# A decoder step on one core: its 344 weight tiles fetched as one 1 MB transfer each in place of two of 512 KB

## The chip, the cores and the metric

The kernel runs on one core of one Trainium2 chip. The metric is the time of one execution on the device in microseconds (us), the median of three runs.

## The reference

One inference step of a one-layer decoder, for 256 prompt tokens and 8 sample tokens, width 2048, all in float32:

```
h    = rmsnorm(x);  proj = h @ w_in                    # 2048 x 7168: conv parts b, c, h and q, k, v, g of 8 heads
y    = [ b * causal_conv3(c*h),  silu(g) * groupnorm(retention(rotary(q), rotary(k), v)) ]
x    = x + y @ w_out                                   # 2048 x 2048
xb   = rmsnorm(x);  q = xb @ w_q                       # 8 heads x 2 x 128
i1, i2 = top16(q0 @ keys0), top16(q1 @ keys1);  best = top16(v1 + v2)   # per token and head
out  = x + sum over the 8*16 picks of softmax(best) * gelu(xb . u[idx]) * v[idx],   idx = 128*i1 + i2
y    = rmsnorm(out);  new conv and retention states are returned too
```

u and v have 16384 rows of 2048. The kernel doesn't gather rows: it multiplies all tokens with all of u, weighs the result with the gates (zero where an expert isn't picked), and multiplies with all of v.

## The kernel before, in words

**Tiles and halves.** All weights (w_in, w_out, w_q, u, v) lie in one DRAM array `halves`, in the order of use. A tile is 16 blocks of 128 x 128 float32, 1 MB; it consists of two halves of 8 blocks, 512 KB, each stored as [128 partitions][8][128], so 4 KB in one piece for a partition. There are 344 tiles, 688 halves, and every half passes once through four steps:

- SP (the queue of `block.sync`) fetches it into one of `RING` = 4 places of `raw` (L520, the first four halves at L504).
- ACT casts it to its high part `whi` (`hi_half`, L607 to L612), once the transfer has landed (`raw_full[s]`) and TensorE has used the half that lay in that place of `whi` before (`half_used`).
- DVE subtracts, raw - whi, to get the low part `wlo` (`lo_half`, L1137), and counts `lo_done`.
- TensorE (`half`, L874 to L884) waits for `lo_done` and runs 24 matmuls of 264 columns: high weight by high and by low activation, low weight by high activation (L881, L882, L883), and counts `half_used`.

**What sets the order.** Nothing is scheduled by a tool: each engine runs a list written out by hand. ACT and DVE call `ahead(r, k)`, which makes the halves 2k+2 and 2k+3 after the tile k is on TensorE, and between two such calls they do the work of the stage: in the eight heads rotation, retention and group norm; then the short convolution; the output projection; queries and scores; then routing (top 16, decoding), and gates, gelu, weighing, and adding. Each engine runs strictly in its order, so what stands behind a cast that waits for its transfer waits too. SP's list is the loop of `fetch` alone after the start: for half m it waits until `lo_done` reaches m - 3, that is, until the low part of half m - 4, which lay in that place, is made.

**The start.** SP issues the norm gains, four blocks of the input x (`acc`, 528 KB each) and halves 0 to 3 between them, and a table (`keep`), then the loop. GpSimd (POOL) waits for the last block of x and then fetches the tables (1584 KB), small constants and the first states (512 KB) over a queue of its own. ACT's list there is `first_squares` (L667 to L682):

```
hi_half(0, 2); hi_half(0, 3)
for c in range(CH):  square of chunk c      # after c == 7: hi_half(0, 4)
hi_half(0, 5); hi_half(0, 6)
root_of_sum(1)
hi_half(0, 7)
ahead(0, 3)                                 # halves 8 and 9
```

and only behind it come the first head's `swap(1)` and `swap(2)` (L644 to L646), which exchange the two halves of k and q for the rotation. DVE's list in the first head (`first_norm`, L1185, and `head`, L1289) makes the low parts of halves 4, 5, 6 and 7 between sums of the squares, then the rotations `rotate(kT...)` and `rotate(qT...)` (L1210 to L1218), then the low parts of halves 8 and 9. On TensorE `turn` (L924), the transposes of v and k for the retention of head 0, comes after tile 3 (halves 6 and 7) and before tile 4 (halves 8 and 9), and waits for both rotations (`rot_ready`).

Of the kernel before, what the change touches and what calls it, by code (L numbers as in the profile page):

```python
# [43 lines left out]
RING = 4  # L44
# [168 lines left out]
def build(nc, halves, xT, conv_state, ret_state, norm_mix, conv_w, gn_g, gn_b, norm_ffn, keysT, norm_fin,  # L213
          consts, out_yT, out_conv, out_pret, out_sret):
    with ExitStack() as ctx:
        def sb(name, shape, dt=F32, scope=ctx):
            return scope.enter_context(nc.sbuf_tensor(name, shape, dt))

        def sem(name):
            return ctx.enter_context(nc.semaphore(name))  # L220


        raw = sb("raw", [P, RING, HALF, P])
# [156 lines left out]
        raw_full = [sem(f"raw_full{s}") for s in range(RING)]  # L380
        hi_done = sem("hi_done")
        lo_done = sem("lo_done")
# [107 lines left out]
        def u_tile(g):  # L490
            return W_U0 if isinstance(g, int) and g == 0 else W_MAIN + (g - 1) * TILES_ROUND

        def v_tile(g):
            last = isinstance(g, int) and g == GROUPS - 1
            return W_MAIN + g * TILES_ROUND + (0 if last else GROUP)


        @block.sync
        def _(sp):
            def x_block(c):  # L500
                sp.dma_start(acc[:, 4 * c:4 * c + 4, :], xT[:, 4 * c:4 * c + 4, :]).then_inc(x_in[c], 16)

            def first_half(s):
                sp.dma_start(raw[:, s], halves[s]).then_inc(raw_full[s], 16)  # L504

            sp.dma_start(gains[:, 0, :], norm_mix).then_inc(gain_in, 16)
            x_block(0)
            first_half(0)
            x_block(1)
            x_block(2)  # L510
            first_half(1)
            x_block(3)
            first_half(2)
            sp.dma_start(keep[:], consts[:, 0:KEEP]).then_inc(keep_in, 16)
            first_half(3)

            def fetch(n, at):
                for s in range(RING):
                    sp.wait_ge(lo_done, n + s - (RING - 1))
                    sp.dma_start(raw[:, s], halves[at + s]).then_inc(raw_full[s], 16)  # L520

            turns = 2 * GROUP // RING
            with sp.Fori(1, 2 * (C_LEAD + GROUP) // RING) as r:
                fetch(r * RING, r * RING)
            with sp.Fori(1, LEAD) as g:
                for i in range(turns):
                    fetch(2 * (C_LEAD + g * GROUP) + i * RING, 2 * u_tile(g) + i * RING)
            with sp.Fori(0, MIXED) as g:
                n = 2 * (C_MAIN + g * TILES_ROUND)
                for i in range(turns):  # L530
                    fetch(n + i * RING, 2 * u_tile(g + LEAD) + i * RING)
                for i in range(turns):
                    fetch(n + 2 * GROUP + i * RING, 2 * v_tile(g) + i * RING)
            with sp.Fori(MIXED, GROUPS - 1) as g:
                for i in range(turns):
                    fetch(2 * (C_TAIL + (g - MIXED) * GROUP) + i * RING, 2 * v_tile(g) + i * RING)
            g = GROUPS - 1
            for i in range(turns):
                fetch(2 * (C_TAIL + (g - MIXED) * GROUP) + i * RING, 2 * v_tile(g) + i * RING)
            for b, (c, n) in enumerate(FINAL):  # L540
                sp.wait_ge(y_out, b + 1)
                sp.dma_start(out_yT[:, c:c + n, :], acc[:, c:c + n, :]).then_inc(stored, 16)
            sp.wait_ge(stored, len(FINAL) * 16)
            sp.wait_ge(conv_stored, 16)
            sp.wait_ge(st_stored, 32 * HEADS)
# [59 lines left out]
        def _(act):  # L605
            def hi_half(r, off):

                s = off % RING
                act.wait_ge(raw_full[s], 16 * (r + off // RING + 1))
                if not (isinstance(r, int) and RING * r + off < RING):  # L610
                    act.wait_ge(half_used, RING * r + off - (RING - 1))
                nc.scalar.copy(whi[:, s], raw[:, s]).then_inc(hi_done, 1)  # L612

            def ahead(r, k):

                hi_half(r, 2 * k + 2)
                hi_half(r, 2 * k + 3)
# [40 lines left out]
            for c in range(CH):  # L658
                if c % 4 == 0:
                    act.wait_ge(x_in[c // 4], 16)  # L660
                times_gains(0, c)
                if c == 3:
                    hi_half(0, 0)
                if c == 11:
                    hi_half(0, 1)
# [143 lines left out]
            for n in range(LEAD_TILES):  # L809
                r, k = C_LEAD // 2, n  # L810
# [49 lines left out]
            r = C_TAIL // 2 + (GROUPS - 1 - MIXED) * (GROUP // 2)  # L860
# [997 lines left out]
```

## Time and profile before

| what | before |
|---|---|
| runs shown | 2143.92 us median of 3 (2143.17 to 2144.35) |
| the profiled execution | 2143.7 us, its span 2142.1 us |
| granted TensorE clock, mean | 0.998 |
| busy: PE / DVE / ACT / POOL | 99% / 66% / 44% / 3% of the span |
| DMA | 414.17 MB, mean 193 GB/s |
| weights, SP's queue | 688 transfers of 512 KB, 3.5 us from issue to landing at the median |

Read the busy shares first, then the chain of work that ended last: both say which engine sets the end. An engine that isn't in the chain may be busy or idle at no cost. For a transfer the question is not how long it takes but whether an engine waited for it, and whether TensorE waited for that engine. In a timeline the brackets at a row's end give how long its engine was idle before it, and who ended that.

### The profile page before, as it was taken

What the parts mean: (1) busy time and instruction counts of PE and PEld (TensorE: products, weight loads), DVE (VectorE), ACT (ScalarE), POOL (GpSimd) and SP (SyncE); (2) the same over time, 40 slices, a digit from 0 to 9 for tenths busy, and PEclk for the clock granted to TensorE, in tenths of its full rate; (3) what the DMA queues carried; (4) which work ended last, traced back from release to release, by engine and by line L of the source; (5) the groups of instructions that cost most, each with busy time, mean ns of one, the idle gap of its engine ahead of it and who ended that gap; (6) DMA issues with size and microseconds to landing.
All of it is one profiled execution on the core that took longest, in us unless ns stands there. A gap on an engine that the chain in (4) does not pass through costs nothing.

```text
span 2142.1 us, 46352 instructions
## 1 busy us (share of the span) xinstructions
PE 2119.1 (99%) x18553; PEld 2101.1 (98%) x18553; DVE 1421.5 (66%) x2684; ACT 941.1 (44%) x1303; POOL 59.7 (3%) x78
## 2 busy tenths in 40 slices
PE   8999999999999999999999999999999999999997
PEld 7999999999999999999999999999999999999997
DVE  7667776568888667754656566666655556666665
ACT  6454433444444434444434343444434344444444
POOL 1000000000010000000000000000000000000000
PEclk9999999999999999999999999999999999999999
DMA  7555555654455556675656665656656566666553
GB/s 276 178 188 179 181 166 179 201 184 151 154 188 181 184 173 217 208 237 194 201 183 213 193 215 184 212 194 201 205 194 202 178 206 212 205 209 206 199 178 127
DMA packets 113767, 414.17 MB, mean 193 GB/s; under 512 B 13216, under 2 KB 13728, under 8 KB 113344
## 3 DMA queue, kind: packets, MB, share of 16 engines
q1 hardware_dynamic: 100800, 365.29, 52.6%
q0 software_dynamic: 8480, 30.24, 4.4%
q10 hardware_dynamic: 4320, 16.22, 1.9%
q8 instruction: 128, 2.10, 0.4%
q14 instruction: 39, 0.32, 0.0%
HBM read 387.36 MB, written 24.26 MB: 192 GB/s over the span
## 4 chain that ended last, share of the span: by engine, by line
PE 98%; DVE 1%; ACT 0%; DMA 0%; issue 0%; DVEq 0%; SPq 0%; ACTq 0%
PE bank L881 31%; PE bank L882 31%; PE bank L883 31%; PE bank L1058 2%; PE bank L959 1%; PE bank L1013 1%; PE bank L948 0%; PE bank L969 0%; DVE wlo L1137 0%; DMA acc<-xT 0%; PE bank L946 0%; DVE acc L1785 0%; PE bank L936 0%; PE bank L965 0%; ACT whi L612 0%
## 5 line engine op out<-in xcount | busy, mean ns | idle before, releaser
L1137 DVE TENSOR_TENSOR wlo<-raw,whi 128x1024 fp32r<-128x1024 f32 x688 | 829.9, 1223 | 537.7 <-ACT whi L612 534.4
L612 ACT CAST whi<-raw 128x1024 fp32r<-128x1024 f32 x688 | 709.6, 1048 | 646.0 <-PE bank L883 636.8
L881 PE MATMUL bank<-xhi,whi 128*128 128x264 f32 x3200 | 911.5, 285 | 0.0
L882 PE MATMUL bank<-xlo,whi 128*128 128x264 f32 x3200 | 906.7, 283 | 0.0
L883 PE MATMUL bank<-xhi,wlo 128*128 128x264 f32 x3200 | 906.5, 283 | 0.0
L882 PEld LDWEIGHTS bank<-xlo,whi 128*128 128x128 f32 x3200 | 603.1, 188 | 0.0
L881 PEld LDWEIGHTS bank<-xhi,whi 128*128 128x128 f32 x3200 | 602.6, 188 | 0.2 <-issue 0.2
L883 PEld LDWEIGHTS bank<-xhi,wlo 128*128 128x128 f32 x3200 | 600.1, 188 | 0.0
L881 PE MATMUL bank<-xghi,whi 128*128 128x264 f32 x1152 | 333.6, 290 | 11.2 <-DVE wlo L1137 11.2
L881 PE MATMUL bank<-wexp_hi,whi 128*128 128x264 f32 x1152 | 328.0, 285 | 0.0
L882 PE MATMUL bank<-xglo,whi 128*128 128x264 f32 x1152 | 327.4, 284 | 0.0
L883 PE MATMUL bank<-xghi,wlo 128*128 128x264 f32 x1152 | 327.0, 284 | 0.0
L882 PE MATMUL bank<-wexp_lo,whi 128*128 128x264 f32 x1152 | 326.4, 283 | 0.0
L883 PE MATMUL bank<-wexp_hi,wlo 128*128 128x264 f32 x1152 | 326.1, 283 | 0.0
L881 PEld LDWEIGHTS bank<-xghi,whi 128*128 128x128 f32 x1152 | 217.9, 189 | 18.0 <-DVE wlo L1137 10.1
L882 PEld LDWEIGHTS bank<-xglo,whi 128*128 128x128 f32 x1152 | 217.8, 189 | 0.4
L882 PEld LDWEIGHTS bank<-wexp_lo,whi 128*128 128x128 f32 x1152 | 217.0, 188 | 0.0
L881 PEld LDWEIGHTS bank<-wexp_hi,whi 128*128 128x128 f32 x1152 | 217.0, 188 | 0.0
L883 PEld LDWEIGHTS bank<-xghi,wlo 128*128 128x128 f32 x1152 | 216.9, 188 | 0.0
L883 PEld LDWEIGHTS bank<-wexp_hi,wlo 128*128 128x128 f32 x1152 | 216.0, 187 | 0.0
L791 ACT ACTIVATE hid<-bank 128x264 f32<-128x264 f32 x128 | 49.8, 389 | 205.3 <-PE bank L883 203.9
L1729 DVE TENSOR_TENSOR acc<-bank,acc 128x264 f32<-128x264 f32 x256 | 99.3, 425 | 49.3 <-PE bank L883 49.3
(215 smaller groups left out, 1102.2 us busy)
## 6 DMA issues: line engine op xcount, KB each, us to landing
raw<-halves SPq DMA_DIRECT2D x688, 512.0 KB, 3.5
hid<-gates ACTq DMA_DIRECT2D x30, 528.0 KB, 4.6
gates<-stage POOLq DMA_DIRECT2D x17, 768.0 KB, 7.1
s_old<-ret_state POOLq DMA_DIRECT2D x8, 512.0 KB, 6.0
ret_sample<-s_new POOLq DMA_DIRECT2D x8, 512.0 KB, 4.1
gates<-route_mem POOLq DMA_DIRECT2D x5, 768.0 KB, 7.2
acc<-xT SPq DMA_DIRECT2D x4, 528.0 KB, 6.4
tables<-shape_constants POOLq DMA_DIRECT2D x1, 1584.0 KB, 8.3
```

The costliest lines, as they stand in the source:

```text
L612: nc.scalar.copy(whi[:, s], raw[:, s]).then_inc(hi_done, 1)
L791: nc.scalar.activation(hid[:, slot_of(g, k)], bank[b][:, 0:T].unsqueeze(1), ACT.Gelu)\
L881: nc.tensor.matmul(out, whi[:, s, c], mh[c], start=start and c == 0, stop=False)
L882: nc.tensor.matmul(out, whi[:, s, c], ml[c], start=False, stop=False)
L883: mm = nc.tensor.matmul(out, wlo[:, s, c], mh[c], start=False, stop=stop and c == HALF - 1)
L959: mm = nc.tensor.matmul(bank[6][:, NPROMPT + b:NPROMPT + b + 1], s_new[:, b], qT[:, NPROMPT + b:NPROMPT + b + 1], start=True, stop=True)
L1013: mm = nc.tensor.matmul(bank[4 + b][0:n, t * NK:(t + 1) * NK], qs[:, b, t0:t0 + n], keys_sb[:, j, :], start=True, stop=True)
L1058: mm = nc.tensor.matmul(o, onehot2[:, e, t], gated1[:, e, part, t], start=part == 0, stop=part == PARTS - 1)
L1137: v.tensor_tensor(wlo[:, s], raw[:, s], whi[:, s].bitcast(F32), ALU.subtract).then_inc(lo_done, 1)
L1729: v.tensor_tensor(acc[:, j, :], bank[off % BANKS][:, 0:T], acc[:, j, :], ALU.add)\
```

## The change

`fetch` walks the ring by two. One transfer fetches both halves of a tile, `raw[:, s:s + 2]`, in a pattern of 128 x 2 x 1024 elements (two pieces of 4 KB for each partition, 512 KB apart in DRAM), and counts on the semaphore of the even place alone. It begins when `lo_done` says that the odd half's place is free too. ACT's cast of an odd half waits for the even place's semaphore, except for halves 0 to 3, which still come one by one.

```diff
             def fetch(n, at):
-                for s in range(RING):
-                    sp.wait_ge(lo_done, n + s - (RING - 1))
-                    sp.dma_start(raw[:, s], halves[at + s]).then_inc(raw_full[s], 16)
+
+                for s in range(0, RING, 2):
+                    sp.wait_ge(lo_done, n + s + 1 - (RING - 1))
+                    sp.dma_start(raw[:, s:s + 2], halves[bass.ds(at + s, 2)].rearrange("s p c k -> p s c k"))\
+                        .then_inc(raw_full[s], 16)
...
             def hi_half(r, off):

                 s = off % RING
-                act.wait_ge(raw_full[s], 16 * (r + off // RING + 1))
+                alone = isinstance(r, int) and RING * r + off < RING
+                act.wait_ge(raw_full[s if alone else s - s % 2], 16 * (r + off // RING + 1))
```

The order of instructions on SP, the last transfer of the start and the first turn of the loop. Before:

```order
L504 DMA raw<-halves 128x1024
L523 UNCONDITIONAL_BRANCH
L523 ISA
L520 ISA [waits lo_done]
L520 DMA raw<-halves 128x1024
L519 REGISTER_ALU
L520 ISA [waits lo_done]
L520 DMA raw<-halves 128x1024
```

With the change:

```order
L504 DMA raw<-halves 128x1024
L525 UNCONDITIONAL_BRANCH
L525 ISA
L521 ISA [waits lo_done]
L521 DMA raw<-halves 128x2x1024
L521 ISA [waits lo_done]
L521 DMA raw<-halves 128x2x1024
```

Each transfer of the loop carries two halves, and there is one wait for `lo_done` for the two.

The order on ACT at the start, from the cast of half 4 to the first swap. Before:

```order
L612 CAST whi<-raw 128x1024 [waits half_used,raw_full0]
L675 ACTIVATE squares<-acc 128x264 [waits sq_used] x8
L612 CAST whi<-raw 128x1024 [waits half_used,raw_full1]
L612 CAST whi<-raw 128x1024 [waits half_used,raw_full2]
L637 ACTIVATE stats<-bank 128x264 [waits sum_done]
L612 CAST whi<-raw 128x1024 [waits half_used,raw_full3]
L612 CAST whi<-raw 128x1024 [waits half_used,raw_full0]
L612 CAST whi<-raw 128x1024 [waits half_used,raw_full1]
L645 COPY swapped<-bank 64x264 [waits half_used]
```

With the change (the lines have moved down by three):

```order
L615 CAST whi<-raw 128x1024 [waits half_used,raw_full0]
L678 ACTIVATE squares<-acc 128x264 [waits sq_used] x8
L615 CAST whi<-raw 128x1024 [waits half_used,raw_full0]
L615 CAST whi<-raw 128x1024 [waits half_used,raw_full2]
L640 ACTIVATE stats<-bank 128x264 [waits sum_done]
L615 CAST whi<-raw 128x1024 [waits half_used,raw_full2]
L615 CAST whi<-raw 128x1024 [waits half_used,raw_full0] x2
L648 COPY swapped<-bank 64x264 [waits half_used]
```

No instruction has moved. The casts of halves 4, 5 and of halves 8, 9 now wait for one transfer each, and the swap still stands behind both casts of the second.

## Rows read from the trace of the kernel before

**Rows 1.** The page: part 1, busy time of each engine, and part 4, chain by engine

```profile
PE 2119.1 (99%) x18553; PEld 2101.1 (98%) x18553; DVE 1421.5 (66%) x2684; ACT 941.1 (44%) x1303; POOL 59.7 (3%) x78
...
PE 98%; DVE 1%; ACT 0%; DMA 0%; issue 0%; DVEq 0%; SPq 0%; ACTq 0%
```

**Rows 2.** Waits of PE: line waited for, us in total, times, longest us

```profile
PE bank L881 <- DVE wlo L1137: 11.2, 2, 9.8
PE bank L913 <- DVE stats L1183: 0.9, 1, 0.9
```

**Rows 3.** Windows (busy us of each engine, PEclk, DMA share, GB/s): a steady stretch

```profile
1570.00:1810.00 240.00, 240.00 (x1989) 240.00 (x1988) 134.01 (x180) 101.02 (x126) 0.00 (x0) 1.00 0.60 197
```

**Rows 4.** Tile raw, whole run: duration ns min/median/max, idle before it, landing

```profile
L612 ACT CAST whi<-raw x688: 1028/1047/1058, 7.5 to 2120.3; 128x1024 fp32r<-128x1024 f32 x172
L1137 DVE TENSOR_TENSOR wlo<-raw,whi x688: 1204/1224/1229, 8.6 to 2121.6; 128x1024 fp32r<-128x1024 f32 x172
...
  DMA raw<-halves: 8.0, 4
...
DMA to landing us min/median/max: 3.1/3.5/9.5
```

**Rows 5.** Tile raw, 119 to 122.5 us: halves 36 and 37, issued back to back

```profile
L520 SPq DMA_DIRECT2D raw<-halves x2: 332/332/333, 120.6 to 121.7; - x2
...
DMA to landing us min/median/max: 3.2/3.7/4.2
```

**Rows 6.** SP's issue of half 5; issues at 14.2 to 15 and 17 to 17.8, us to landing

```profile
14.34 0.34 SPq L520 DMA_DIRECT2D raw<-halves  x1
...
raw<-halves SPq DMA_DIRECT2D x1, 512.0 KB, 7.6
...
raw<-halves SPq DMA_DIRECT2D x1, 512.0 KB, 8.2
```

**Rows 7.** Windows of the start, DMA share and GB/s last

```profile
14.00:16.00 2.00, 2.00 (x18) 2.00 (x18) 2.00 (x6) 1.97 (x3) 2.00 (x5) 1.00 1.06 429
22.00:24.00 2.00, 2.00 (x19) 2.00 (x18) 1.68 (x3) 1.60 (x5) 0.00 (x0) 1.00 1.02 342
```

**Rows 8.** Timeline of ACT, start: start us, us, line, tile [idle before, releaser]

```profile
19.35 1.03 ACT L612 CAST whi<-raw 128x1024 fp32r<-128x1024 f32 x1
...
29.03 1.05 ACT L612 CAST whi<-raw 128x1024 fp32r<-128x1024 f32 x1 [0.22 <-DMA raw<-halves]
30.38 1.06 ACT L612 CAST whi<-raw 128x1024 fp32r<-128x1024 f32 x1 [0.30 <-PE bank L883]
31.46 0.38 ACT L645 COPY swapped<-bank 64x264 f32<-64x264 f32 x1
...
41.49 1.05 ACT L612 CAST whi<-raw 128x1024 fp32r<-128x1024 f32 x1 [3.63 <-DMA raw<-halves]
```

**Rows 9.** Timeline of DVE, start: low part of half 5, and qT

```profile
24.85 1.23 DVE L1137 TENSOR_TENSOR wlo<-raw,whi 128x1024 fp32r<-128x1024 f32 x1
...
35.43 0.43 DVE L1218 TENSOR_TENSOR qT<-qT,rot 128x264 f32<-128x264 f32 x1
```

**Rows 10.** Timeline of PE, start: first matmul of the turn

```profile
36.01 0.41 PE L928 MATMUL bank<-keep,vT 128*128 128x128 f32 x2
```

**Rows 11.** Timelines of SP, ACT and PE near 284 us

```profile
284.61 0.33 SPq L520 DMA_DIRECT2D raw<-halves  x1
...
286.89 1.06 ACT L612 CAST whi<-raw 128x1024 fp32r<-128x1024 f32 x1 [3.68 <-DMA raw<-halves]
...
283.45 0.36 PE L881 MATMUL bank<-xghi,whi 128*128 128x264 f32 x1 [1.37 <-DVE wlo L1137]
```

**Rows 12.** Windows at the first matmuls and at the end, granted clock after POOL

```profile
9.80:13.90 4.10, 4.05 (x18) 4.05 (x19) 4.10 (x9) 4.10 (x10) 1.36 (x3) 1.00 1.03 416
2131.00:2133.00 2.00, 0.80 (x4) 0.34 (x2) 0.71 (x2) 0.49 (x2) 0.00 (x0) 1.00 0.00 0
2133.00:2135.00 2.00, 0.00 (x0) 0.00 (x0) 1.93 (x4) 0.00 (x0) 0.00 (x0) 0.66 0.00 0
```

## The prediction

> **What bounds the kernel now.** I read the page first. TensorE is busy for 99% of the span, and the chain that ended last runs over it for 98% [rows 1]. Nothing that an engine, a queue or a transfer saves elsewhere shortens the span; only what makes TensorE wait, or wait less, counts. The waits of TensorE come next: two on a finished low part (DVE, L1137), together 11.2 us, 9.8 of which are the start before the first matmul, and 0.9 us at the end [rows 2]. So the weights arrive in time everywhere but once, for 1.4 us, and the change can win almost nothing. The question is where it makes TensorE wait.
>
> A steady stretch gives the pace: 1989 matmuls in 240.00 us, 0.1207 us each, 24 to a half, so 2.90 us for a half and 5.8 us for a tile [rows 3]. A half costs ACT 1.05 us (high part) and DVE 1.22 us (low part); a transfer lands in 3.5 us at the median and 9.5 at most, and in the whole run ACT's casts wait for a transfer four times, 8.0 us in all [rows 4]. Halves are numbered from 0 in their order of use.
>
> **What the change does to a transfer.** The even half of a pair no longer starts when its own place is free but when the odd one's is, and both are there only when 1 MB has landed. Nothing before half 4 is touched, and no instruction of PE, DVE, ACT or POOL moves; SP issues 342 transfers in place of 684. That saves 342 issues on a queue that only waits: nothing.
>
> No row has a 1 MB transfer on this queue, so its landing time is bounded. Two halves issued 1.13 us apart (120.6 and 121.7) took 3.2 to 4.2 us, so the pair was complete about 1.1 + 4.2 = 5.3 us after the first issue, 5.4 with rounding [rows 5]. That is the upper end. The lower end is the quiet single landing, 3.2 to 3.3 us, plus 0.5 MB at the 429 GB/s that the engines reached when full [rows 7], 1.2 us: 4.5 us. I take 4.9, between them, since one transfer has no second start but the same bytes. The Trainium skill (DMA: Bandwidth & Descriptors, "Anatomy of one DMA") gives a fixed 2.0 us and the bytes at 436 GB/s: 3.2 us for half a megabyte, with which the trace agrees, and 4.4 us for one; the sum below would be 0.5 us smaller by it. Its table of measured sizes on another issue path has 6.15 us for 1 MB, by which the sum would be 1.2 us larger; no row here has that size.
>
> **Steady stretches: nothing.** A place pair is held from the issue to the end of the second low part: the landing, 0.2 us of issue, two casts and one low part, 1.0 + 1.0 + 1.2, so 4.9 + 3.4 = 8.3 us. There are two such pairs and TensorE eats one in 5.8 us, so each may take 11.6 us. 3.3 us are left. The one place after the start where ACT waited for a transfer is half 80: half 81 was issued at 284.61, half 80 just before it, and the cast of half 80 began at 286.89 [rows 11]. As a pair they land near 284.6 + 4.9 = 289.5, and the low part of half 80 ends at 289.5 + 2.3 = 291.8. TensorE started half 76 at 283.45 and reaches half 80 four halves later, at 295.1. The 1.4 us wait ahead of half 76 hangs on a chain of DVE work and stays.
>
> **The start: this is the term.** The places are filled while inputs and constants crowd the same engines.
> - Halves 4 and 5. Half 5 is issued at 14.34 as before, half 4 (at 9.97 before) now with it. Half 5 landed 7.6 us later, at 21.9; half 6, issued at 17.09, took 8.2 and landed at 25.3 [rows 6]. The engines are full from 14 to 16 us (share 1.06, 429 GB/s), and move 342 GB/s from 22 to 24 [rows 7]. With full engines the same bytes pass whichever goes first, so the pair is complete near 21.9. Below: 0.5 MB less stands ahead of the constants and all come 1.2 us sooner, 20.7. Above: it shares with 0.5 MB more at 342 GB/s, 1.5 us later, 23.4. I take 22.1, since GpSimd's constants, issued from 12.5, get the room that half 4 leaves.
> - ACT casts half 4 at 19.35 now [rows 8]. It does so at 22.1, 2.75 us later. Behind that cast in ACT's order stand eight squares and the cast of half 5, behind it on DVE the sums of the squares. The low part of half 5 ended at 24.85 + 1.23 = 26.08 [rows 9], 6.7 us after the cast of half 4 began, with hardly a gap between; so it ends at 28.8. TensorE waits for these two halves, 1 to 2 us in all.
> - Halves 8 and 9 are issued when that low part ends: 28.8 + 0.2 = 29.0. Half 8 alone went out after the low part of half 4 and was there at 29.03 [rows 8]. The pair lands at 29.0 + 4.9 = 33.9, with a quiet queue, since half 6 is in at 25.3 and half 7, the 9.5 us of [rows 4], soon after.
> - ACT casts halves 8 and 9 ahead of the two half-swaps of the first head (L645). Before, the casts began at 29.03 and 30.38 and the first swap at 31.46 [rows 8]; now the casts begin at 33.9 and 34.9 and the swap at 35.9, 4.4 us later. DVE's rotation waits for it: qT was ready at 35.43 + 0.43 = 35.86 [rows 9], and TensorE's turn (L928) began at 36.01, the moment it was [rows 10]. There was no room at all. DVE's multiply stood 1.0 us behind the first swap because of other work, now long done; 0.4 us of the 4.4 come back.
> - Sum for TensorE: 22.1 + 6.7 + 0.2 + 4.9 = 33.9, less 29.9: the 29.03 of the old cast, the 0.5 us that shrink between cast and swap (2.4 before, when the cast of half 9 waited for TensorE, 2.0 now) and the 0.4 that come back. That is +4.0 us. With both lower ends +2.2 (20.7 and 4.5), with both upper ends +5.8 (23.4 and 5.4).
> - Halves 12 and 13 are issued after the low part of half 9, which follows the rotation: 40.0 + 2.4 = 42.4, landed at 47.5, half 12 cast and its low part made by 49.8 (its cast began at 41.49 [rows 8]). TensorE starts half 8 after the turn, past 41 now, and half 12 four halves later, not before 52.6: nothing added.
>
> TensorE never has idle time later in which to catch up, so the 4.0 us stay to the end. The profiled execution took 2143.7 us beside a span of 2142.1 and a median of the runs of 2143.92, the same within 0.01%. 2143.9 + 4.0 = **2147.9 us**, +0.19%. A difference of 0.2%, 4.3 us, is about what a measurement of this kernel can tell from none; the forecast lies just inside it.
>
> **Rivals.**
> 1. Slower by more than 0.2%: the same mechanism with a late pair. It decides once landing time of halves 4 and 5 and the quiet landing together exceed 27.3 us (22.1 + 4.9 = 27.0 in the forecast). For it: half 6 landed only at 25.3, since GpSimd's transfers took turns with it. Against it: they are through sooner. With 23.4 and 5.4 it gives +5.8, 2149.7 us.
> 2. The stall cools the clock. At the end TensorE's last matmul lies in 2131 to 2133, at the full clock (2.4 GHz); in 2133 to 2135 the granted mean is 0.66, so it fell to half (1.2 GHz) 0.6 us into that stretch, within 2.6 us of work [rows 12]. The new wait near 38 us is the rest of the 4.0, 2 to 3 us. For it: that may be as long. Against it: the 1.4 us gap near 283 was followed by the full clock, and here the work before and after is dense. At the start 18 matmuls took 4.10 us, 0.228 each [rows 12], 0.107 more than in the steady stretch (that row grants 1.00, but the pace is that of the lower level); 18 of them again are +1.9: 2149.8 us.
> 3. Steady starvation. If the pair needed 9 us, the places would be held 9 + 3.4 = 12.4 of 11.6 us, 0.8 too much for each of 172 double tiles: +138 us, 2282 us. From 8.2 us it decides. For it: the longest single landing is 9.5. Against it: that one is in the crowd of the start, and the median is 3.5.
> 4. No loss, or a gain. Either the pair is split so that its first half is as early as before, or larger transfers are much quicker. The Trainium skill (same page, "Rules for kernel authors") asks for at least 1 MiB in a transfer for full bandwidth. On the rows, quicker landings could win back the 1.4 us near 283 at most: 2142.5 to 2143.9 us.
>
> **How the numbers follow.** Forecast 0.50, rival 1 0.32, rival 2 0.05, rival 3 0.05, rival 4 0.08 (0.05 of it no difference, 0.03 faster by an unseen way). Slower by over 0.2%: 0.32 + 0.05 + 0.05 = 0.42; within: 0.50 + 0.05 = 0.55; faster: 0.03. The range starts at the lower ends, +2.2, rounded to 2146.0, and takes in the upper ends with the clock, 5.8 + 1.9 = 7.7: 2151.6. Rivals 3 and 4, 0.13, lie outside.
>
> **What would show it.** The cast of half 4 at 22 with a wait on the transfer in place of 19.35; the casts of halves 8 and 9 near 34, with some 4 us of waiting; waits of TensorE of 1 to 2 us on low parts between 23 and 29, and one of 2 to 3 us at the turn (L928, three lines lower in the new file) that ends near 40; landings of 4.6 to 5.4 us at the median; every stretch after 60 us as long as before. I am wrong if TensorE waits on low parts in later stretches, if the median landing is above 6 us, or if the first head starts its turn before 38 us.

## The result, and the profile after

| what | before | with the change |
|---|---|---|
| runs | 2143.92 us median of 7 (2143.17 to 2144.35) | 2149.83 us median of 7 (2149.39 to 2151.58) |
| the profiled execution | 2143.7 us, span 2142.1 us | 2149.74 us, span 2148.2 us |
| granted TensorE clock, mean | 0.998 | 0.997 |

The ratio is 1.003, with an interval of 1.0019 to 1.0041: 5.9 us slower, 0.28%. The forecast said 4.0, the range 2.1 to 7.7; the time is that of rival 1, the late pair. It is also past the 0.2% within which the prediction expected the change to stay (0.55, against 0.42 for slower than that). Five of the seven runs lie within 1.3 us (2149.39 to 2150.63), two at 2151.45 and 2151.58.

The waits of PE in the changed kernel (line waited for, us in total, times, longest us), against [rows 2]:

```profile
PE bank L884 <- DVE wlo L1140: 14.3, 3, 9.7
PE bank L931 <- DVE qT L1221: 1.5, 1, 1.5
PE bank L916 <- DVE stats L1186: 0.9, 1, 0.9
```

One wait on a low part has been added and one on the rotation. The window of [rows 3] and a longer one up to the end of the weights, with the granted clock before the last two numbers:

```profile
1570.00:1810.00 240.00, 240.00 (x2006) 239.95 (x2005) 133.02 (x177) 100.99 (x126) 1.16 (x1) 1.00 0.58 198
590.00:2130.00 1540.00, 1539.53 (x13881) 1535.33 (x13881) 997.90 (x1739) 663.12 (x875) 35.22 (x40) 1.00 0.58 197
```

TensorE is as full as before (2006 matmuls against 1989: a few per cent of the records can be missing). So nothing is lost later, and all of the loss lies in the first 42 us. There the chain reads, on ACT (start us, us, line, tile, and in brackets how long ACT was idle before it and who ended that):

```profile
23.89 1.04 ACT L615 CAST whi<-raw 128x1024 fp32r<-128x1024 f32 x1 [4.64 <-DMA raw<-halves]
28.33 1.99 ACT L615 CAST whi<-raw 128x1024 fp32r<-128x1024 f32 x2
...
35.63 2.00 ACT L615 CAST whi<-raw 128x1024 fp32r<-128x1024 f32 x2 [2.41 <-DMA raw<-halves]
37.65 0.38 ACT L648 COPY swapped<-bank 64x264 f32<-64x264 f32 x1
```

on DVE, where the two low parts at 29.39 are those of halves 5 and 6:

```profile
24.97 1.23 DVE L1140 TENSOR_TENSOR wlo<-raw,whi 128x1024 fp32r<-128x1024 f32 x1 [4.80 <-ACT whi L615]
29.39 2.36 DVE L1140 TENSOR_TENSOR wlo<-raw,whi 128x1024 fp32r<-128x1024 f32 x2
...
38.51 0.43 DVE L1218 TENSOR_TENSOR kT<-bank,tables 128x264 f32<-128x264 f32 x1 [1.52 <-ACT swapped L649]
...
41.49 0.43 DVE L1221 TENSOR_TENSOR qT<-qT,rot 128x264 f32<-128x264 f32 x1
```

and on PE:

```profile
26.25 0.39 PE L884 MATMUL bank<-xghi,whi 128*128 128x264 f32 x1 [3.25 <-DVE wlo L1140]
...
31.49 0.48 PE L884 MATMUL bank<-xghi,whi 128*128 128x264 f32 x1
...
42.07 0.41 PE L931 MATMUL bank<-keep,vT 128*128 128x128 f32 x2 [1.53 <-DVE qT L1221]
```

The turn began at 36.01 [rows 10] and begins at 42.07: +6.06. Every half from 8 on is 6.05 to 6.08 us later, and the span is 6.1 us longer.

The two landings that the sum of the prediction holds, from the DMA issues of 14 to 15 us and of 30.5 to 31.5 us (KB, us to landing):

```profile
raw<-halves SPq DMA_DIRECT2D x1, 1024.0 KB, 9.7
...
raw<-halves SPq DMA_DIRECT2D x1, 1024.0 KB, 4.8
```

And tile `raw` in the whole run, us to landing:

```profile
DMA to landing us min/median/max: 4.7/4.9/9.8
```

The quiet landing is 4.9 us, as taken. That of halves 4 and 5 is 9.7, from 14.15 to 23.87, where 7.8 (14.34 to 22.1) was taken. Why it is so long is in the queues' shares of the engines (queue, packets, MB, share of 16 engines; q1 is SP's, q0 GpSimd's), of 14.5 to 18 us, then 18 to 21, then 21 to 24:

```profile
q0 software_dynamic: 102, 1.29, 92.7%
q1 hardware_dynamic: 4, 0.00, 0.3%
...
q1 hardware_dynamic: 208, 0.85, 74.4%
q0 software_dynamic: 206, 0.26, 24.8%
...
q0 software_dynamic: 142, 0.50, 53.4%
q1 hardware_dynamic: 141, 0.51, 47.7%
```

GpSimd issued its tables (1584 KB) at 12.32, the pair was issued at 14.15, and for almost four microseconds it moved hardly a byte. About two of these four a pair takes even alone. The quiet pair 8/9 was issued at 30.80, and these are its rows of 31 to 32, 32 to 33 and 33 to 34 us:

```profile
q1 hardware_dynamic: 13, 0.05, 68.0%
q1 hardware_dynamic: 28, 0.11, 41.9%
q1 hardware_dynamic: 110, 0.45, 109.3%
```

It was in full flow 2.2 us after its issue. From 18 to 21 us the pair 4/5 had three quarters of the engines, and from 21 on about half, beside the first states, which GpSimd had issued at 16.21. The engines weren't full all the time either. The window of 14 to 16 us, where half 4 was among what passed before (429 GB/s, [rows 7]), now reads:

```profile
14.00:16.00 2.00, 2.00 (x19) 2.00 (x18) 2.00 (x5) 2.00 (x3) 2.00 (x5) 1.00 1.03 337
```

**The clock.** The windows from TensorE's wait before half 4 to the end of the next halves:

```profile
22.90:26.50 3.60, 0.34 (x3) 0.26 (x3) 1.53 (x2) 2.31 (x5) 0.00 (x0) 1.00 0.84 305
26.50:29.90 3.40, 3.40 (x17) 3.40 (x17) 2.94 (x5) 2.96 (x6) 0.00 (x0) 0.50 0.02 8
29.90:33.00 3.10, 3.10 (x24) 2.96 (x23) 2.50 (x4) 1.53 (x3) 0.00 (x0) 1.00 0.35 54
```

After 3.25 us without a matmul, the granted clock was 0.50 for 3.40 us, which is 1.2 GHz. In the timeline the matmuls of that stretch begin 0.22 us apart (the count of 17 takes in those that its edges cut), where 0.12 is usual. In this execution that costs little: TensorE waits for qT at the turn in any case, and what half 4 took longer (half 5 is late by 4.45 us where half 4 was by 2.81, so 1.6) is missing from the wait at the turn, 1.5 instead of about 3.

### The profile page after: what moved, and what is told of

Its sections match the earlier page's. It is cut to its first block, busy times and chain, and to the rows that moved or that the text cites. A ratio compares the mean times of both kernels' runs of the same rounds, so it can differ in the third digit from the quotient of the medians.

```text
span 2148.2 us, 45008 instructions
## 1 busy us (share of the span) xinstructions
PE 2120.6 (99%) x18553; PEld 2102.3 (98%) x18553; DVE 1421.3 (66%) x2684; ACT 940.7 (44%) x1303; POOL 59.7 (3%) x78
## 4 chain that ended last, share of the span: by engine, by line
PE 97%; DVE 1%; DMA 1%; ACT 0%; issue 0%; DVEq 0%; SPq 0%; ACTq 0%
PE bank L884 31%; PE bank L885 31%; PE bank L886 30%; PE bank L1061 2%; PE bank L962 1%; PE bank L1016 1%; DMA raw<-halves 0%; DVE wlo L1140 0%; PE bank L951 0%; PE bank L972 0%; DMA acc<-xT 0%; ACT whi L615 0%; PE bank L949 0%; DVE acc L1788 0%; PE bank L939 0%
```

## The experiments

Every kernel was timed beside the kernel before on the same chip; before had medians of 2143.91 (e1 to e4), 2144.03 (e5 to e8) and 2143.81 (e9 to e12). The theory: the whole loss is made at the start, by two links in a chain, the pair 4/5 that comes late and the pair 8/9 whose casts stand ahead of the swaps. The rivals: it is made in the steady part by tight places; or it is the clock; or a single one of the two links makes it.

### Where: the steady part or the start

In e1 and e2 `fetch` chooses between a pair and two single halves, each with the wait of its own kernel, and ACT's wait follows it (`one` and `two` hold the two forms of the transfer; SP's first two turns stand ahead of its loop). e1 begins with pairs at half 12; e2 has pairs for halves 4 to 11 alone.

```diff
+            def fetch(n, at, first=()):
+                for s in range(0, RING, 2):
+                    if (n + s in FIRST) if isinstance(n, int) and n < 3 * RING else STEADY:
+                        sp.wait_ge(lo_done, n + s + 1 - (RING - 1))
+                        two(s, at)
+                    else:
+                        for t in (s, s + 1):
+                            sp.wait_ge(lo_done, n + t - (RING - 1))
+                            one(t, at)
```

> Pairs from half 12 on only; halves 4 to 11 come one by one as before. Start theory (the whole loss is made by the pairs 4/5 and 8/9): no difference from before, 2143.9 +- 0.5 us, no wait of TensorE beside the three of before. Rival (part of the loss is spread over steady stretches): +0.5 us or more, with new waits of TensorE on low parts after 60 us.

Measured: 2143.7 us (2143.14 to 2144.59, 11 runs), ratio 0.9999 (0.999 to 1.0008). ACT's waits for a transfer (whole run) grow from 4 to 20 and cost nothing, since PE's are those of [rows 2] but for 0.1 us:

```profile
ACT whi L634 <- DMA raw<-halves: 53.9, 20, 6.5
PE bank L903 <- DVE wlo L1159: 11.3, 2, 9.9
```

So 338 pairs change the time by no more than 0.1% either way. The steady rival falls.

> Pairs for halves 4 to 11 only, singles from half 12 on. Start theory: all of the loss, +5.9 us, 2149.8, with the wait before half 4 and the wait at the turn as in the changed kernel. Rival of a spread loss: clearly less than +5.9.

Measured: 2150.4 us (2148.62 to 2151.37), ratio 1.0029 (1.0019 to 1.0039): four pairs are the whole loss. In its profile the clock fell in another place. The turn's first matmul,

```profile
41.59 0.41 PE L950 MATMUL bank<-keep,vT 128*128 128x128 f32 x2 [2.28 <-DVE qT L1240]
```

and the windows from before the turn to half 9:

```profile
36.00:42.90 6.90, 4.62 (x39) 4.41 (x38) 4.23 (x11) 4.63 (x8) 0.00 (x0) 1.00 0.33 135
42.90:46.30 3.40, 3.40 (x17) 3.40 (x17) 3.40 (x5) 0.52 (x2) 0.00 (x0) 0.51 0.62 181
```

Here nothing waits behind the slow stretch. The halves are 5.6 us late before it and 7.1 after it, so this time the clock is on the path, for 1.5 us. That is rival 2 as the prediction described it.

### Which pair

e3 has `FIRST = (4,)` and e4 `FIRST = (8,)` in the same code, all others single.

> Only halves 4 and 5 come as a pair. They land near 23.9 us, TensorE starts half 5 4.4 us later than before, and the cast of half 8 waits for nothing, since half 8 goes out after the low part of half 4 (26.2) and is there near 30. Theory of two links (late 4/5, then late 8/9): +4.4 if the half-rate clock after the wait is repeated, +2.8 if it is not. Rival (4/5 alone does it all): +5.9.

Measured: 2147.6 us (2146.93 to 2148.75), ratio 1.0018 (1.0009 to 1.0027): +3.7, between the two values expected (2.8 and 4.4). In its profile the clock stayed full.

> Only halves 8 and 9 come as a pair, issued after the low part of half 5, 26.07 + 0.2 = 26.3, landed 4.9 later at 31.1. The cast of half 8 begins 2.1 us later than before and 0.4 to 0.5 of that comes back at the swap: theory of two links +1.5 to +1.6 us, with one wait of TensorE at the turn. Rival (the landing has room here): 0.

Measured: 2145.3 us (2144.95 to 2145.43), ratio 1.0006 (0.9997 to 1.0016): +1.4, which the interval does not tell from nothing; the trace does. ACT's casts of halves 8 and 9, then the first swap, in e4:

```profile
31.16 2.00 ACT L634 CAST whi<-raw 128x1024 fp32r<-128x1024 f32 x2 [2.11 <-DMA raw<-halves]
33.18 0.38 ACT L667 COPY swapped<-bank 64x264 f32<-64x264 f32 x1
```

The swap stood at 31.46 [rows 8]: 1.7 us earlier. The pair was issued at 26.28, after the low part of half 5, and half 8 alone had gone out after that of half 4. So the two links are worth 3.7 and 1.4, and together 5.9 or 6.5, some 1 us over their sum.

### Late start, or larger transfer

e5 keeps the change's wait but sends two single halves.

```diff
-                    sp.dma_start(raw[:, s:s + 2], halves[bass.ds(at + s, 2)].rearrange("s p c k -> p s c k"))\
-                        .then_inc(raw_full[s], 16)
+                    for t in (s, s + 1):
+                        sp.dma_start(raw[:, t], halves[at + t]).then_inc(raw_full[t], 16)
```

> Every tile comes as two transfers of 512 KB with a semaphore each, but both are issued when both places are free: the late start without the one large transfer. Half 4, issued at 14.2, lands when half 5 did before, near 21.9, half 5 near 23.7; the low part of half 5 ends near 28.6, half 8 lands 3.3 us after its issue at 28.8, half 9 near 33.4, and the first swap comes near 34.5 in place of 31.46. Start theory: +2.9 us (2146.8): the late start and the size each carry about half of the loss. Rival (the late start is all): +5.9. Rival (the size is all): 0.

Measured: 2146.16 us (2145.75 to 2146.92), ratio 1.0009 (1.0 to 1.0019): +2.1, expected 2.9. The casts of half 4, then of halves 8 and 9:

```profile
21.89 1.05 ACT L614 CAST whi<-raw 128x1024 fp32r<-128x1024 f32 x1 [2.45 <-DMA raw<-halves]
...
32.09 1.05 ACT L614 CAST whi<-raw 128x1024 fp32r<-128x1024 f32 x1 [2.11 <-DMA raw<-halves]
33.38 1.05 ACT L614 CAST whi<-raw 128x1024 fp32r<-128x1024 f32 x1 [0.23 <-DMA raw<-halves]
```

The cast of half 4 went from 19.35 to 21.89 by the later start and from there to 23.89 by waiting for 1 MB: 2.5 and 2.0 us. In the profiled execution (2146.58 us) the turn begins at 38.88, 2.9 us late. So a third to a half of the whole loss is the later start (2.1 to 2.9 of 5.9), the rest the size of what is waited for.

### Taking the links away, one by one

e6 takes the casts of halves 8 and 9 out of the way of the swaps; all transfers stay pairs.

```diff
                 hi_half(0, 7)
-                ahead(0, 3)
...
-                if loads_tiles(h) and not first:
+                if loads_tiles(h):
                     ahead(r, 3)
```

> The changed kernel, with ACT's casts of halves 8 and 9 put behind the two half-swaps of the first head. The pair 8/9 still lands near 35.5, but the rotation no longer waits for it. Theory (the loss of the second pair goes through ACT's order): what is left is the late pair 4/5, as in the run that paired only these, +3.7 us, 2147.6; the wait at the turn falls under 0.5 us. Rival (TensorE would wait for half 8 itself): +5.9.

Measured: 2147.93 us (2146.75 to 2148.79), ratio 1.0018 (1.0009 to 1.0027): +3.9. TensorE's wait at the turn fell to 0.2 us. What is left is the price of the pair 4/5, as in e3.

e7 makes GpSimd wait with its tables until halves 0 and 4/5 are in.

```diff
-            pool.wait_ge(x_in[3], 16)
+            pool.wait_ge(raw_full[0], 32)
```

> The changed kernel, with GpSimd's first transfers (tables, constants, first states, 2.2 MB) held back until halves 4 and 5 have landed. Theory (the pair is late because it shares the engines with them): it lands in 5 to 5.5 us, near 19.5 in place of 23.9, its cast is on time, and only the second pair is late, 26.4 + 4.9 to 7 us: +1.8 to +3.8 us, 2146.1 likeliest. Rival (the wait for both places is the cause, not the company): the pair lands at 23 or later and the loss stays at +5.9.

Measured: 2148.94 us (2148.33 to 2150.11), ratio 1.0022 (1.0012 to 1.0032): +4.9. The time is a miss, the reading of the crowd is not. Landings of the pairs 4/5 and 8/9 (issued at 13.83 and 25.75):

```profile
raw<-halves SPq DMA_DIRECT2D x1, 1024.0 KB, 4.8
...
raw<-halves SPq DMA_DIRECT2D x1, 1024.0 KB, 8.0
```

ACT's cast of half 8 and the first matmul of the turn:

```profile
33.76 1.99 ACT L615 CAST whi<-raw 128x1024 fp32r<-128x1024 f32 x2 [5.79 <-DMA raw<-halves]
...
40.20 0.64 PE L931 MATMUL bank<-keep,vT 128*128 128x128 f32 x2 [4.90 <-DVE qT L1221]
```

and the windows up to the start of half 8, and of half 8:

```profile
36.00:42.20 6.20, 2.00 (x10) 1.91 (x11) 4.91 (x10) 3.26 (x6) 0.00 (x0) 0.84 0.01 3
42.20:45.90 3.70, 3.70 (x27) 3.70 (x27) 3.70 (x8) 0.52 (x2) 0.00 (x0) 0.81 0.67 205
```

With GpSimd's transfers out of its way, the pair 4/5 takes 4.8 us where it took 9.7, and half 4 is no longer late. But the tables now meet the pair 8/9, which takes 8.0, and TensorE waits 4.9 us at the turn in one piece. The rotation waited for the swap and not for the tables that it reads: DVE waited 4.3 us for the swap there, and 0.5 us for GpSimd's constants, by 30.17. The clock falls there too: 0.84 and 0.81 are 1.0 us and 0.7 us less than full, as 3.4 us at half would make them, and half 8 takes 3.7 us in place of 3.0.

e9 joins both edits: the tables late and the swaps ahead.

> The changed kernel with both repairs: GpSimd's first transfers after halves 4 and 5, and ACT's casts of halves 8 and 9 behind the two half-swaps. The pair 4/5 lands near 18.7 as in the run with late tables, the pair 8/9 near 33.7 (it meets the tables), in time for a cast that begins near 34. Theory (the loss consists of these two waits and nothing else): 2144.0 to 2145.0, the time of before plus 0 to 1 us. Rival (something else in the pairs costs time at the start): +2 us or more.

Measured: 2143.68 us (2143.12 to 2144.94), ratio 1.0 (0.9991 to 1.001), with pairs everywhere. PE's waits on low parts, then ACT at the start:

```profile
PE bank L883 <- DVE wlo L1139: 11.4, 2, 10.0
```

and

```profile
19.53 1.03 ACT L615 CAST whi<-raw 128x1024 fp32r<-128x1024 f32 x1
...
29.29 0.38 ACT L648 COPY swapped<-bank 64x264 f32<-64x264 f32 x1
```

Half 4 is cast at 19.53 without a wait and the swap no longer stands behind a transfer. The loss is gone, within the 2 us that the interval allows, and the trace has no wait of TensorE left at the start after the first matmul: the two links are all of it. The two repairs weren't run with single halves, but there they have no wait to remove, since TensorE doesn't wait between its first matmul and 283 us before the change [rows 2].

### The clock's part

e8 runs 12 matmuls that nothing reads before half 4 and 12 before head 1's turn in PE's list, that is, in the two waits. They are extra work.

```diff
+                    if first and k == 2:
+                        pe.wait_ge(keep_in, 16)
+                    if first and k == 2 or isinstance(h, int) and h == 1 and k == 0:
+                        for _ in range(12):
+                            nc.tensor.matmul(bank[7][:, 0:P], ones, ident, start=True, stop=True)
```

> The changed kernel, with 12 small matmuls into an unused bank ahead of half 4 and 12 ahead of the first turn (extra work, its results are not read). They fill some 2.6 us of the two waits. Theory (the runs of the changed kernel above 2150 us are those in which the clock fell in the wait at the turn and half 8 ran at half rate): no stretch at half clock before the end, no run above 2150.2, the median 2149.5. Rival (the spread comes from the landing of the transfers): the spread stays, 2149.4 to 2151.6.

Measured: 2149.89 us (2149.41 to 2150.79, 8 runs), ratio 1.0027 (1.0016 to 1.0038). The window of its start:

```profile
22.00:45.00 23.00, 22.62 (x185) 21.84 (x184) 16.11 (x27) 13.01 (x23) 0.00 (x0) 1.00 0.45 154
```

The clock stayed at 1.00 (2.4 GHz) throughout, and the median is that of the changed kernel. The expected values, a median of 2149.5 and no run above 2150.2, were both missed: two of the eight runs lie above (2150.30 and 2150.79). So the clock is no part of the typical loss; the chain of transfers, casts and rotation sets it, whatever TensorE does meanwhile. The highest run came down from 2151.58 to 2150.79, but the runs still spread over 1.4 us. That the two slowest runs of the changed kernel are those in which the clock fell on the path, as in e2's profile, fits, but with eight runs it isn't shown.

### What could still be won, and how near the edge is

The wait of 1.4 us ahead of half 76 is there in both kernels. e10 is the kernel before with DVE's low parts of halves 76 and 77 at the head of their channel's work instead of near its end; e11 is e9 with the same.

```diff
                 conv_ahead(3 * j)
+                if j == 1:
+                    conv_ahead(3 * j + 2)
...
-                conv_ahead(3 * j + 2)
+                if j != 1:
+                    conv_ahead(3 * j + 2)
```

> The kernel before (singles), with DVE's low parts of halves 76 and 77 put at the head of the second channel of the convolution in place of its middle. They are ready near 281 in place of 283.3, and the one wait of TensorE in mid-run, 1.4 us near 283, goes. Theory: -1.2 to -1.4 us, 2142.7. Rival (the channel's chain is late next and the wait moves behind it): 0.

> The changed kernel (pairs) with both repairs of the start and the early low parts of halves 76 and 77. If the three act apart: the time of the run with both repairs less 1.2 to 1.4 us, about 2143, the same as the singles with early low parts within 1 us. If larger transfers had a gain of their own anywhere, it would lie below these singles.

Measured: e10 2142.05 us (2141.55 to 2143.29, 11 runs), ratio 0.9992 (0.9983 to 1.0001), 1.8 us less than before; e11 2142.62 us (2141.5 to 2143.04, 11 runs), ratio 0.9993 (0.9984 to 1.0002). The intervals just reach 1, but in e10's trace the wait is gone:

```profile
PE bank L881 <- DVE wlo L1137: 10.1, 1, 10.1
```

With pairs or with single halves the repaired kernel takes the same time within 0.6 us. Pairs bring nothing of their own.

e12 begins every pair one half later.

```diff
-                    sp.wait_ge(lo_done, n + s + 1 - (RING - 1))
+                    sp.wait_ge(lo_done, n + s + 2 - (RING - 1))
```

> The changed kernel, with every pair begun one half later still (it waits for the low part of the next half too). In stages where ACT casts the next tile only when TensorE has finished one, that half comes a whole tile later, 5.8 us: a place is then held 4.9 + 3.4 + 5.8 = 14.1 us, of 11.6 that there are. Theory of the margin (3.3 us in the changed kernel, and 2.5 too much here): 2.5 us for each of 172 double tiles, +430 us, near 2570. Rival (the margin is much larger than 3.3 us): under +100 us.

Measured: 2655.03 us (one run), +511 us where +430 was expected. The half that it now waits for lies in the other pair of places, so a pair can't start before the one ahead of it has landed. The casts of three pairs in a row:

```profile
1604.58 2.00 ACT L615 CAST whi<-raw 128x1024 fp32r<-128x1024 f32 x2 [4.94 <-DMA raw<-halves]
1612.05 2.00 ACT L615 CAST whi<-raw 128x1024 fp32r<-128x1024 f32 x2 [5.47 <-DMA raw<-halves]
1619.96 1.99 ACT L615 CAST whi<-raw 128x1024 fp32r<-128x1024 f32 x2 [5.43 <-DMA raw<-halves]
```

and the window of [rows 3]:

```profile
1570.00:1810.00 240.00, 204.04 (x1783) 198.87 (x1779) 119.62 (x188) 78.67 (x106) 4.61 (x4) 0.97 0.47 160
```

That is a pair every 7.5 us or more, where TensorE eats one in 5.8. The mean clock is 0.97 in this window, so it falls in some of the waits too. Starvation in every tile, as rival 3 has it, would look like this, though here the pairs are kept apart and their landing is as quick as before; the change itself keeps clear of it by the one half.

## Why the prediction was right, and where it was short

- **Steady stretches: nothing.** Right, and shown by e1 (2143.7 against 2143.91). The slowest pair took 8.3 us in 1570 to 1810 us, past the 8.2 from which rival 3 would decide if all did; the 3.3 us of room that each pair has carried it.
- **342 issues saved: nothing.** Right: the same e1, and e11 against e10.
- **The quiet landing, 4.9 us.** Right to 0.1: 4.8 for the pair 8/9, 4.9 at the median. By the formula of the Trainium skill (DMA: Bandwidth & Descriptors, "Anatomy of one DMA") it would have been 4.4, and by its table 6.15. The page gives both for transfers issued from GpSimd, and these are SP's. The trace bears out neither: 1 MB took 4.7 at the quickest, and 512 KB took 3.5 at the median [rows 4] where the formula has 3.2.
- **Landing of halves 4 and 5, 22.1 us.** This is the term that failed: 23.87, past even the upper end of 23.4. The step "with full engines the same bytes pass whichever goes first" was wrong. From 14 to 16 us 0.18 MB less passed than before (337 GB/s in place of 429), and what passed was mostly GpSimd's: q0 had 92.7% of the engines from 14.5 to 18 us. Issued ahead of the tables, at 9.97, half 4 had landed after 6.6 us, by 16.6; behind them the pair moved next to nothing until near 18, then met the first states. From 18 to 24 us q1 moved 1.36 MB, of which the pair is 1.05: the next pair, issued at 18.04, took some of the room too. e7 shows the cause: 4.8 us with GpSimd's transfers held back.
- **6.7 us from that cast to the end of half 5's low part.** Right: 23.89 to 29.39 + 1.22 = 30.61 is 6.7. TensorE's waits were split otherwise than foretold: 3.25 us before half 4 where 1 to 2 were expected for halves 4 and 5, and 1.53 at the turn where it was 2 to 3.
- **The swaps behind the casts of 8 and 9, no room at the turn.** Right: e6 (+3.9 in place of +5.9) and e9 show it. But 0.4 us were to come back between swap and rotation, and 0.1 did: the swap is 6.19 us later than at 31.46, the turn 6.06.
- **The sum with what was measured**: 23.87 + 6.74 + 0.19 + 4.81 = 35.61, less 29.03 + 0.4 + 0.13 = 29.56 is 6.05, the 6.06 of the trace. Of the 2 us missing in the forecast, 1.8 are the landing and 0.3 what didn't come back; the other terms are each off by 0.1 and cancel.
- **Rival 1** took its place by its own condition: 23.9 + 4.8 = 28.7 is over 27.3. Its chance, 0.32, was too small beside 0.50: the evidence for it stood in [rows 6], where half 6, issued 2.8 us later, took 8.2.
- **Rival 2** came true in part: the clock did fall, in half 4 in the changed kernel's profile, where the turn's wait covers it, and behind the turn in e2's, where it costs 1.5.
- **Rival 4**, no loss or a gain: the steady pairs bring none (e1, and e11 against e10), and the start costs.
- **Halves 12 and 13, and the 1.4 us at 283: nothing.** Right: all later halves are late by the same 6.05 to 6.08, and the wait is there at 289.50 with 1.38 us.

## What to carry to other kernels

A transfer of twice the size costs twice in latency: it starts later, since it needs more free room, and its first byte is of use only when its last has landed. In a steady pipeline that is held against the room of each place and may cost nothing; at the start, where an engine's fixed list puts the cast ahead of work that the bound engine waits for, each microsecond goes to the end. So work out the first two turns of a ring by themselves, and ask of each early transfer which other queue's transfers it was ahead of and will now be behind.

A repair that moves a crowd must be followed to its new place: the tables out of the way of one pair stood in the way of the next, and only both repairs together paid.

## What the runs showed of the hardware

- Two queues didn't share the full engines evenly at once: a 1 MB transfer, issued 1.8 us after a 1584 KB one of GpSimd's, began to move near 18 us, 3.7 us after its issue, while the other queue had 92.7% of the engines from 14.5 to 18. The quiet pair 8/9 was in full flow 2.2 us after its issue, so the crowd held the other back by about 2 us. Whether its bytes were ready to go earlier isn't shown. Later, against the 512 KB of states, the two queues had 53% and 48%.
- 1 MB landed in 4.9 us at the median and 512 KB in 3.5 [rows 4], so the second half megabyte costs 1.4 us in one transfer; as two transfers, back to back, the pair took about 5.3 [rows 5].
- The clock fell after waits of TensorE of 3.25 us (the changed kernel, before half 4) and 2.28 (e2, at the turn, 1.3 us into the work after it), and in e7 about when the turn began, after 4.90; it did not after 2.52 (e6) and 1.38 (before half 76). In the first two cases it stayed down for 3.4 us, and matmuls began 0.22 us apart in place of 0.1207 [rows 3]. The length of one wait alone doesn't order these cases; in e2 there had been a wait of 1.80 us before half 4 as well. What does stays open.
